# Dilated attention of a two-layer model: the mask added by VectorE on the way from bank to memory

## What is computed

```python
DIL_PATTERNS = ((128, 1), (512, 4), (2048, 16))
def dilated_branch(q, k, v, dilation, wc):
    ...
    s = jnp.einsum('brhnqd,brhnkd->brhnqk', qc, kb).astype(jnp.float32) * (dh ** -0.5)
    ...
    valid = (dist >= 0) & (dist <= wc) & ((blk > 0) | (j >= wc))
    s = jnp.where(valid, s, -jnp.inf)
    lse = jax.nn.logsumexp(s, axis=-1)
    p = jnp.exp(s - lse[..., None])
    o = jnp.einsum('brhnqk,brhnkd->brhnqd', p.astype(vb.dtype), vb)
...
    wts = jax.nn.softmax(jnp.stack(lses, axis=0), axis=0)
    o = jnp.sum(wts[..., None].astype(v.dtype) * jnp.stack(outs, axis=0), axis=0)
    return o.reshape(B, S, ODD_MIX) @ w_out
```

## Time and profile before

| | us |
|---|---|
| median of 3 runs | 3302.1 (3300.92 to 3303.79) |
| profiled execution | 3302.35 |
| its span | 3300.5 |
| TensorE busy | 3254.2 |
| VectorE busy | 1906.7 |
| ScalarE busy | 1277.2 |
| GpSimd busy | 807.0 |
| mean granted clock of TensorE | 0.999 |

### The profile page before, as it was taken

The page is one execution under the profiler, slowest core; times in us unless marked ns, Lnnn a source line. Parts: engine busy times, 40 slices in busy tenths (PEclk is TensorE's granted clock), DMA queues, the critical chain, the costliest instruction groups (busy, mean ns, idle before and its releaser), DMA issues.

```text
span 3300.5 us, 47729 instructions
## 1 busy us (share of the span) xinstructions
PE 3254.2 (99%) x17192; PEld 2761.1 (84%) x17192; DVE 1906.7 (58%) x2532; ACT 1277.2 (39%) x1930; POOL 807.0 (24%) x501
## 2 busy tenths in 40 slices
PE   8989999999999999999999999999999999999999
PEld 6769888988888888998888978888898888898887
DVE  6577767554577666576645676664553355363333
ACT  5364433354554334543222555322242223442221
POOL 1111222110112222532322141232223231113321
PEclk9999999999999999999999999999999999999999
DMA  4203433321234333455534311453432243222222
GB/s 154 77 33 115 146 132 129 112 96 63 77 110 156 130 140 115 178 181 191 193 143 172 126 52 45 158 186 147 159 109 89 102 164 110 103 90 91 100 97 95
DMA packets 70187, 401.63 MB, mean 122 GB/s; under 512 B 7680, under 2 KB 10384, under 8 KB 31632
## 3 DMA queue, kind: packets, MB, share of 16 engines
q1 hardware_dynamic: 46544, 317.80, 27.0%
q10 hardware_dynamic: 23488, 81.73, 7.0%
HBM read 397.41 MB, written 2.10 MB: 121 GB/s over the span
## 4 chain that ended last, share of the span: by engine, by line
PE 95%; DVE 2%; issue 1%; ACT 1%; DMA 0%; DVEq 0%; SPq 0%; ACTq 0%
PE banks L551 25%; PE banks L552 25%; PE banks L553 25%; PE banks L473 3%; PE banks L474 3%; PE banks L475 3%; PE banks L592 1%; PE banks L594 1%; PE banks L593 1%; PE banks L994 1%; PE banks L957 1%; PE banks L712 1%; PE banks L982 1%; PE banks L871 1%; PE banks L683 0%
## 5 line engine op out<-in xcount | busy, mean ns | idle before, releaser
L551 PE MATMUL banks<-h_hi,whi 128*128 128x512 f32 (+1 forms) x2736 | 1032.9, 378 | 3.3 <-DVE wlo L1662 1.3
L553 PE MATMUL banks<-h_hi,wlo 128*128 128x512 f32 (+1 forms) x2736 | 1027.4, 376 | 0.0
L552 PE MATMUL banks<-h_lo,whi 128*128 128x512 f32 (+1 forms) x2736 | 1027.3, 375 | 0.0
L2451 POOL TENSOR_TENSOR wlo<-raw,whi 128x512 fp32r<-128x512 f32 (+1 forms) x281 | 441.8, 1572 | 2175.9 <-ACT whi L1069 2175.9
L551 PEld LDWEIGHTS banks<-h_hi,whi 128*128 128x128 f32 x2736 | 515.0, 188 | 102.5 <-issue 8.7
L552 PEld LDWEIGHTS banks<-h_lo,whi 128*128 128x128 f32 x2736 | 515.1, 188 | 93.3 <-issue 1.7
L553 PEld LDWEIGHTS banks<-h_hi,wlo 128*128 128x128 f32 x2736 | 515.0, 188 | 93.3
L1069 ACT ACTIVATE whi<-raw 128x1024 fp32r<-128x1024 f32 x281 | 296.4, 1055 | 561.3 <-PE banks L553 517.8
L1662 DVE TENSOR_TENSOR wlo<-raw,whi 128x1024 fp32r<-128x1024 f32 x281 | 467.7, 1664 | 39.5 <-ACT whi L1071 39.5
L551 PE MATMUL banks<-mid_hi,whi 128*128 128x512 f32 (+1 forms) x1136 | 423.6, 373 | 2.3 <-issue 2.3
L553 PE MATMUL banks<-mid_hi,wlo 128*128 128x512 f32 (+1 forms) x1136 | 423.2, 373 | 0.0
(11 more groups left out here) (323 smaller groups left out, 4004.9 us busy)
## 6 DMA issues: line engine op xcount, KB each, us to landing
raw<-stream SPq DMA_DIRECT2D x297, 1024.0 KB, 4.8
mraw<-mod_stream ACTq DMA_DIRECT2D x144, 512.0 KB, 3.4
x<-xT SPq DMA_DIRECT2D x8, 256.0 KB, 6.6
out<-x SPq DMA_DIRECT2D x8, 256.0 KB, 2.0
ka<-k_a ACTq DMA_DIRECT2D x1, 1600.0 KB, 6.9
ko<-k_odd ACTq DMA_DIRECT2D x1, 1152.0 KB, 5.0
raw<-stream SPq DMA_DIRECT2D x2, 512.0 KB, 5.7
crow<-c_rows ACTq DMA_DIRECT2D x1, 1024.0 KB, 4.9
```

Source lines behind the costliest of these rows:

```text
L551: mm(o, hi, a_hi[:, kc, 0:T], start=(kc == 0), stop=False)
L552: mm(o, hi, a_lo[:, kc, 0:T], start=False, stop=False)
L553: last = mm(o, lo, a_hi[:, kc, 0:T], start=False, stop=(kc == K - 1))
L2451: G.tensor_tensor(wlo[:, slot, 0:wd], raw[:, slot, 0:wd], whi[:, slot, 0:wd].bitcast(F32), ALU.subtract)\
```

## The change

VectorE adds the mask table to the scores while it takes them from the banks to `oP`, and the maximum and the exponential read `oP` (the exponential in place). TensorE writes no masks: the score products start their banks themselves. score(n) waits until unit n-2 has been added (`odd_masked`). The add waits until the weights of the unit that last used its half of `oP` are done, and the maximum waits for the add's own semaphore. The table holds the 768 columns of a unit together, once for each residue (3072 columns instead of 2304), and the cast to `ko_r` is gone.

```diff
-KO_NEAR, KO_G1, KO_G2, NODD = 0, 2048, 2048 + P, 2304
+ODD_KEYS = S + 2 * P
+NODD = 4 * ODD_KEYS
...
+        odd_masked = sem("odd_masked")
...
                 def score(n):
-                    if n >= n0 + 2:
+                    if n >= n0 + 2 and name == "even_in":
                         pe.wait_ge(sems["probs"], n - 1)
+                    elif n >= n0 + 2:
+                        pe.wait_ge(odd_masked, n - 1)
                     scores(n, acc[(n + last_slab + 1) % 2]).then_inc(sems["scores"], 1)
...
                 def odd_scores(n, dst):
                     hh, r = ODD_U[n % 8]
-                    mask(dst[0], ko_r[:, KO_NEAR + r * S:KO_NEAR + (r + 1) * S])
-                    mask(dst[1][:, 0:2 * P], ko_r[:, KO_G1:KO_G1 + 2 * P])
-                    onto_mask(dst[0], oq[:, hh, r * P:(r + 1) * P], okk[:, hh, :])
+                    mm(dst[0], oq[:, hh, r * P:(r + 1) * P], okk[:, hh, :], start=True, stop=True)
                     for g in (1, 2):
-                        last = onto_mask(dst[1][:, (g - 1) * P:g * P], oq[:, 2 * g + hh, r * P:(r + 1) * P],
-                                         okk[:, 2 * g + hh, r * P:(r + 1) * P])
+                        last = mm(dst[1][:, (g - 1) * P:g * P], oq[:, 2 * g + hh, r * P:(r + 1) * P],
+                                  okk[:, 2 * g + hh, r * P:(r + 1) * P], start=True, stop=True)
                     return last
...
-                    pe.wait_ge(masks_ready, 5)
...
-                        last = A(p_ap[:, b, c * S:c * S + w], scores[:, c * S:c * S + w], ACT.Exp,
+                        src = scores if ncomp == 2 else p_ap[:, b, :]
+                        last = A(p_ap[:, b, c * S:c * S + w], src[:, c * S:c * S + w], ACT.Exp,
...
-                    src = pairs[k][:, :, 0:nblocks(n) * P] if ncomp == 2 else flat[k][:, 0:768]
+                    if ncomp == 2:
+                        src = pairs[k][:, :, 0:nblocks(n) * P]
+                    else:
+                        at = ODD_U[n % 8][1] * ODD_KEYS
+                        if n >= 2:
+                            dve.wait_ge(sems["weights"], n - 1)
+                        src = p_ap[:, b, :]
+                        V.tensor_tensor(src, flat[k][:, 0:ODD_KEYS], ko[:, at:at + ODD_KEYS], ALU.add)\
+                            .then_inc(odd_masked, 1)
+                        dve.wait_ge(odd_masked, n + 1)
...
-                        V.tensor_copy(ko_r[:], ko[:]).then_inc(masks_ready, 1)
```

More of the change, by code:

```diff
@@ L255, in build @@
                           ("dP", [P, 2, 2 * S]), ("dW", [P, 2, S]), ("dWT", [P, 2, S])])
-        oq, okk, ov, ko, ko_r, oP, oW, oWT, oo = scope([
-            ("oq", [P, 6, S]), ("okk", [P, 6, S]), ("ov", [P, 3, TT, 256]), ("ko", [P, NODD]), ("ko_r", [P, NODD], F32R),
+        oq, okk, ov, ko, oP, oW, oWT, oo = scope([
+            ("oq", [P, 6, S]), ("okk", [P, 6, S]), ("ov", [P, 3, TT, 256]), ("ko", [P, NODD]),
             ("oP", [P, 2, 768]), ("oW", [P, 2, 768]), ("oWT", [P, 2, 768]), ("oo", [P, 4, S])])
@@ L2685, in constants @@
         dist = (r + 4 * p)[:, None] - (4 * (t % P) + t // P)[None]
[L2686 to L2689, removed]
+        at = r * ODD_KEYS
+        odd[:, at:at + S] = np.where((dist >= 0) & (dist <= 128), 0.0, NEG)
+        n = p[:, None] - p[None]
+        odd[:, at + S:at + S + P] = np.where(n >= 0, 0.0, NEG)
+        odd[:, at + S + P:at + ODD_KEYS] = np.where((n >= 0) & (n % 4 == 0), 0.0, NEG)
     a = np.zeros((P, NA), np.float32)
```

## The result

The changed kernel took **3312.24 us** (median of 12 runs, 3304.91 to 3315.30) beside 3304.24 us for the kernel before (12 runs, 3299.77 to 3306.68): ratio **1.0022**, 95% interval 1.0014 to 1.0030. That is slower by 0.2%, above the bound of 3308.7 and above the top of the range (3310). The page hardly moved; TensorE lost a percent of its share.

What follows compares the result with a forecast made beforehand. TensorE, busy 99% of the span, was taken as the bound, with VectorE's queue deciding at the ends of a pass. 3302.35 + 1.6 order of work + 2.8 clock = 3306.75, so a median of 3306.5 us; range 3301 to 3310.

Steps and rivals of the forecast that it cites:

- The start: Start of a pass: VectorE's two adds ahead of unit 1's weights delay its transposes by 1.56 us.
- The add: VectorE, per unit: one add of 768 columns takes 0.95 us, bounds 0.69 and 1.55; maximum starts 0.99 after it.
- Rival 2: VectorE becomes the bound: adds towards 1.55 us, deciding from about 1.24; +3.6 us a pass, 3313.7; chance 0.12.
- The steady part: Transposes of unit 1 to unit 5: four scores lose their masks, 3.22 us a unit, -1.72 us a pass.
- The end: End of a pass: VectorE's queue delays unit 6's transposes, 3.30 us after unit 5's instead of 2.00, +1.30 us.
- Order of work: Both passes, sum without clock loss: -0.35 + 1.56 - 1.72 + 1.30 = +0.79 us a pass, +1.6 for both.
- The clock: Behind each pass's 4.0 us idle: 3.4 us at half speed, costing 1.4 us a pass, bounds 0 and 2.5.
- rival 1: Behind the start's gap: clock stays up or half speed lies inside the gap; 3303.7 us, chance 0.26.
- The starting point: Whole kernel before: profiled execution 3302.35 us, 0.25 above the runs' median, so the forecast stood on 3302.1.
- The range: Whole kernel: 3301 to 3310 us, from clock loss of 0 to 2.5 a pass and the runs' own 1.5 either way.
- my own sign: Whole trace: time moved outside the two stretches 741 to 779 and 876 to 914 would make the reasoning wrong.
- rival 3: Both passes: products simply gone, VectorE's added work hides everywhere; -6.7 us, 3295.4; chance 0.04.

Runs made afterwards that it cites:

- the first comparison: The changed kernel against the kernel before, 12 runs each, ahead of two repetitions: 3312.24 us beside 3304.24, ratio 1.0022.
- the split at the end: Changed kernel with VectorE's split of the next slab's weights moved behind the last unit: 3304.71 us, ratio 0.9999 to the kernel before.
- two products: Changed kernel with two unused TensorE products a pass placed in the gap before unit 1's transposes: 3308.34 us, ratio 1.0013 to the kernel before.
- the kernel with the weights first: Changed kernel with VectorE doing the weights of unit n ahead of add and maximum of unit n+1: 3309.89 us, ratio 1.0016 to the kernel before.
- the interleaved order: Changed kernel with unit n's weights between add and maximum of unit n+1, next slab's split behind the last unit: 3301.07 us, ratio 0.9992; repeated, 3301.33.

## Why the prediction was right and wrong

**The start** was right: +1.56 us predicted, 7.98 and 8.06 us measured from score 1 to the transposes of unit 1, so +1.61 and +1.69, released by VectorE's scaling behind an idle of 3.73 us, where I had 4.0.

**The add** was right at 0.95 (0.956 over 16), as was the step of 0.99 to the maximum. Rival 2 falls with it: no add reached 1.24 us. Even the one whose first 0.38 us ran beside GpSimd's split (753.52 to 754.79) took 0.96. That is what the Trainium skill's page "SBUF — State Buffer", section "SBUF: two separate sides", says of an operation with one operand in a bank. The maximum stayed at 0.953 from memory, where it had 0.96 and 0.95 from the bank; the 0.065 us that the Trainium skill's page "VectorE: DVE Perf Modes", section on the TRN2 errata, would have given back (an estimate from its two fixed costs) did not come.

**The steady part** was too good by 0.08 us a unit: I took a unit as 3.65 less the 0.43 of its masks, and 0.08 us of the masks had cost nothing. Four units in two passes make 0.6 us. The cast that went took 1.35 us in the trace before (L2209), not the 2.4 that I gave; the sum had it at nothing.

**The end** was right in kind and slightly too dear: 3.15 us from unit 5 to 6, +1.15 instead of +1.30.

Order of work together: about +1.05 a pass, **+2.1** instead of +1.6. The runs at equal clock say 1.6 to 2.0.

**The clock** fell in both passes as forecast, and rival 1 with its 3303.7 is out. The first step that failed is "I take 1.4 a pass". A fall of 3.4 us costs 1.6, since nearly all of it lies behind the gap, and two of the six falls lasted about twice as long and cost 2.8 to 2.9, beyond my upper bound of 2.5 as well. The mean is 2.04: **+4.1** instead of +2.8. My reading that 2.40 us of idle do nothing and 3.12 us bring the fall was too simple as well: the trace that I had shows a fall behind 1.31 us (0.75 in the window 190 to 195).

**The starting point** was 1.3 us too low: the forecast stood on 3302.1, the median of three runs; 107 runs have a median of 3303.4.

With these three, 3303.4 + 2.1 + 4.1 = 3309.6, which is the median of the 34 runs. That it agrees to the tenth is luck, with a clock term from three profiles. It also lies inside my range.

**The range** is the second step that failed, and it is what put 3312.24 outside: the term "the runs' own 1.5 us below and above", taken from three runs. The changed kernel's runs differ by 0.995 to 0.998 in mean clock, 8 us in time by the table above, and the first comparison had mostly the low clocks. Behind that stands what the clock does elsewhere, of which I had said nothing: the 2.86 us lost ahead of the passes in the profiled execution are that. By my own sign (time moved outside 741 to 779 and 876 to 914) the reasoning was wrong there: it put the clock outside the passes at nothing. Against the forecast of 3306.75 that execution took 3311.38 us; of the 4.6 us some 0.6 are order of work, 1.7 the falls in the passes and 2.3 elsewhere. Inside the passes the mechanism was right, and of the clock's term only the size was off.

The products are gone, the gain is real (-5.3 us alone, of which the trace places 4.1), and so rival 3 was half of the story; the other half is the price of the add at the ends of a pass.

## What to carry to other kernels

Work that moves from a full engine to a half-empty one is paid at the places where the full engine waits for the other: follow the second engine's queue there, not its busy share. Put the operations that release someone first and those that only start a chain after them, but never so that the engine waits out a round trip through a third one. Then follow the time saved to the next place where the full engine waits: part of it can end there. A gap of a few microseconds on TensorE is to be costed with what the clock loses behind it, from gaps of that length in the same trace, and runs are best compared at equal granted clock.

## What the hardware showed that was not expected

- The same program, same chip, ran at mean granted clocks of 0.996 to 0.999 (before) and 0.995 to 0.998 (changed), and its time followed at 2.5 to 3 us per 0.001. The median of each group of 29 or 33 runs was steady to 1.2 us all the same (3304.3, 3303.1, 3303.2).
- Of idle stretches just before the transposes of unit 1, 3.73 us was followed by half clock six times in six, 3.13 and 3.22 us twice in two; 2.0 us once in four (the split at the end and two products, two passes each). What tells the falls of 3.4 us from those of twice the length stays open.
- In the kernel with the weights first an idle of 1.88 us ahead of unit 1 was followed by a fall in the second pass, and in the kernel before one of 1.31 us at 192. So length alone doesn't decide; no run here tells what else does.
- A fall ahead of a wait for another engine can cost little. In the interleaved order's profile the clock stands at 0.56 and 0.58 from 938 to 942, and TensorE's next wait (for `h_lo`, VectorE, at 942.35) shrank to 0.24 us from 1.74 in the kernel before.
- Taking away 0.43 us of products that stood at the start of a unit shortened the unit by 0.35 us.
- The exponential of 768 columns takes 0.936 us from memory (median of 16) where it took 0.898 from the bank.
